# The second output projection as two pairs of column chunks with seven block products each

## The chip, the cores and the metric

The kernel runs on one core of one Trainium2 chip, as one launch. The metric is the device time of that launch in microseconds (us), given as the median of several executions. The profile comes from one more execution, recorded by the hardware profiler; its own time stands beside its span below.

## The reference, cut to what matters

Two transformer blocks run one after the other on 256 tokens of width 2048, in float32. The change touches only this step of the second block, and its result feeds the feed-forward layer behind it:

```
merged = gate_a * (y_a @ w_branch_a) + gate_b * (y_b @ w_branch_b)   # 256 x 2048
x = x + merged @ w_out                                               # 256 x 2048 times 2048 x 2048
x = x + swiglu(rms_norm(x, norm_ffn), w_gate_up, w_down)
```

## The kernel before, in words

Every matrix product is made in float32 precision from three matmuls in a faster format. A weight is split into a high part (`whi`, written by ScalarE with a copy that rounds) and the rest (`wlo`, written by VectorE as raw minus high part). The activations are split in the same way and are the stationary operand. A product of one 128-row tile is then high·high + high·low + low·high, three matmuls of 512 columns into one bank of PSUM.

The unit of work is a *piece*: 256 rows by 512 columns of a weight (128 partitions x 1024 elements). The helper `piece` issues 12 matmuls for it: 2 row tiles (`k`) x 2 token tiles (`i`) x 3. Pieces are numbered through the whole kernel by `g`. Their high and low parts live in a ring of four slots, `whi[:, g % 4]` and `wlo[:, g % 4]`. Three counters order them: `hi_ready` (ScalarE has made the high part of piece g), `lo_ready` (VectorE has made the low part) and `piece_used` (TensorE is through with it). ScalarE waits for `piece_used >= g - 3` before it writes the high part of piece g, so both splitting engines run at most some three pieces ahead of TensorE. The raw weights arrive in four units `raw[:, u]` of 1 MB, two pieces each; SyncE issues the load of a unit when VectorE is through with both pieces that it held (`quad`).

Each engine has its own program, written out by hand in one order. Work beside the splits is hooked in after a numbered piece j of a block of eight (a *block* is one column chunk of 512 columns: 8 pieces over the 2048 rows). The second output projection (`Q_WO2`) is four such blocks, c = 0 to 3, that alternate between the two pairs of accumulator banks, `acc[1]` and `acc[0]`. Around it:

- before it, the last mix block (`Q_MIX + 7`, products with the branch weights) ends in `acc[0]`; VectorE's `branch_b(3)` (L573) multiplies that result by a gate and adds it to `gates`, after piece 2 of c = 0;
- TensorE transposes results in groups of four 128x128 tiles, two groups before piece 4 of a block (`late`, `LATE`); after piece 6 ScalarE and VectorE turn them into stationary operands (`stat_group`): for the merged activations `mhi`, `mlo`, for the residual `hboth` and `rows_of`;
- `h2_add(c - 1)` (L2175) adds the finished chunk to the residual `xres`, on VectorE after piece 2 of the next block; `h2_squares` (L1621) squares it on ScalarE;
- behind it, two blocks of the feed-forward layer (`Q_FF`), then ten loop bodies. The bodies already make part of their gate and up products as seven block products instead of eight (`into`, `right_sum`, `combine`), with a ring of six slots.

Of the kernel before, what the change touches and what calls it, by code (L numbers as in the profile page):

```python
# [33 lines left out]
P = 128  # L34
D = 2048
KT = D // P
TOK = 256
# [33 lines left out]

ORDER = (("a", 0), ("b", 0), ("g", 0), ("c", 0), ("v1", 0), ("g", 1), ("v2", 0), ("u", 0), ("v3", 0),
# [7 lines left out]
B0 = 8 * Q_BODY  # L80
# [97 lines left out]
LATE.update({Q_WO2 + 1 + c: G_H2 + 2 * c for c in range(4)})  # L178
# [29 lines left out]
def build(nc, t, out):  # L208
# [3 lines left out]
    with ctx:  # L212
# [82 lines left out]
        mlo = place("mlo", [P, KT, TOK], F32R, at=o_r + 16384)  # L295
        bias2 = place("bias2", [P, HEADS2, TOK], at=o_ybuf)
# [35 lines left out]

        def raw_piece(u, half):

            return (raw[:, u] if u < 4 else raw2[:, u - 4])[:, 2 * half:2 * half + 2, :]

        def ring(x, odd):

            slot = (NB * odd + x) % SLOTS
            return (whi[:, slot], wlo[:, slot]) if slot < 4 else (whi2[:, slot - 4], wlo2[:, slot - 4])  # L340
# [79 lines left out]
        tile_done = sem("tile_done")  # L420
        h2_added, h2sq, h2var, h2rstd = sem("h2_added"), sem("h2sq"), sem("h2var"), sem("h2rstd")
# [17 lines left out]
        def use_taken(n):  # L439
# [12 lines left out]
            if n < U_FF:  # L452
                return h2_added, n - U_WO2 + 1
            return (ff_silu, 1)

        def late(pe, q, j, transpose_group, aux_bank, aux_used):
# [3 lines left out]
            for s in (LATE[q], LATE[q] + 1):  # L460
# [17 lines left out]
                else:  # L478
                    pe.wait_ge(h2_added, (s - G_H2) // 2 + 1)
# [28 lines left out]
        def late_slot(w, late, j):  # L508

            return late[:, j] if j < 4 else w[:, j - 4]  # L510
# [62 lines left out]
        def branch_b(dve, chain, c):  # L573
# [4 lines left out]
            chain.after(chain.step(nc.vector.tensor_tensor(gate_now[:], pair[(U_MIX + 3 * c + 2) % 2][:], gate_now[:], ALU.mult)))  # L578
            y = gates[:, :, c * CW:(c + 1) * CW]
            nc.vector.tensor_tensor(y, y, gate_now[:], ALU.add).then_inc(merged, 1)  # L580
# [3 lines left out]
        def _(pe):  # L584
# [438 lines left out]
            for c in range(4):  # L1023
                q, n = Q_WO2 + c, U_WO2 + c
                for j in range(8):
                    g = 8 * q + j
                    late(pe, q, j, transpose_group, aux_bank, aux_used)
                    if c == 0 and j % 2 == 0:
                        pe.wait_ge(stat_ready, G_MERGED + j + 2)
                    if j == 0:  # L1030
                        pe.wait_ge(*use_taken(n - 2))
                    pe.wait_ge(lo_ready, g + 1)
                    piece(g % 4, j == 0, j == 7, acc[n % 2], m_stat, 2 * j)
# [10 lines left out]
            for c in range(2):  # L1044
                q = Q_FF + c
                for j in range(8):
                    g = 8 * q + j
# [144 lines left out]
        def _(sp):  # L1192
# [4 lines left out]
            def quad(q, srcs):  # L1197

                for u in range(4):
                    sp.wait_ge(lo_ready, 8 * (q - 1) + 2 * u + 2)  # L1200
# [75 lines left out]
            for c in range(4):  # L1276
                quad(Q_WO2 + c, column_block(t["w_out_2"][0], c * CW))
            quad(Q_FF, column_block(wgu, 0))
            quad(Q_FF + 1, column_block(wgu, DFF))

            def load(i, what, r, u):
# [8 lines left out]
                elif isinstance(i, int) and i == 0:  # L1290
                    if u >= 4:
                        sp.wait_ge(piece_used, 8 * Q_FF)
                    else:
                        sp.wait_ge(lo_ready, 8 * (Q_FF + 1) + 2 * u + 2)
# [26 lines left out]
        def _(act):  # L1321
            chain = Chain(act, act_steps)

            def split(q, j):

                g = 8 * q + j
# [13 lines left out]
                nc.scalar.activation(whi[:, j % 4], raw[:, j // 2, 2 * (j % 2):2 * (j % 2) + 2, :], ACT.Copy).then_inc(hi_ready, 1)  # L1340
# [266 lines left out]
            for c in range(4):  # L1607
                for half_q in range(2):
                    q = Q_MIX + 2 * c + half_q
                    for j in range(8):  # L1610
# [3 lines left out]
                        if half_q == 1 and j == 3:  # L1614
                            sigmoid_b(act, c)
                        if q in LATE and j == 6:
# [4 lines left out]
            def h2_squares(k):  # L1621
                act.wait_ge(h2_added, k + 1)
# [20 lines left out]
            for c in range(4):  # L1643
                q = Q_WO2 + c
                for j in range(8):
                    split(q, j)
# [948 lines left out]
```

## Time and profile before

| what | value |
|---|---|
| time, median of 3 runs | 1731.69 us (1731.48 to 1732.12) |
| the profiled execution's own time | 1731.04 us |
| its span, first to last instruction | 1729.2 us |
| TensorE busy | 1714.8 us, 99% |
| VectorE busy | 1246.7 us, 72% |
| ScalarE busy | 953.1 us, 55% |
| second output projection, first to last matmul | 939.39 to 1030.06 us |

PE is TensorE's matmul side, PEld its weight loads, DVE is VectorE, ACT ScalarE, SP SyncE. Lines such as L1783 are lines of the kernel file. Times in the timeline count from the first instruction. A timeline row can join several instructions of one kind: then its duration runs from the first one's start to the last one's end, and the count stands behind it. An instruction that follows another on its engine without a wait starts a little before the end that the profile gives for the other.

### The profile page before, as it was taken

Reading aid. Unit: us, or ns where it says so; the run is one execution under the profiler, and the core shown is the slowest. Engines: PE = TensorE matmul, PEld = TensorE weight load, DVE = VectorE, ACT = ScalarE, POOL = GpSimd, SP = SyncE. Lnnn points to the kernel's source line nnn. Section 1 sums busy time; section 2 is a strip of 40 time slices with the busy share of each in tenths; the row PEclk is TensorE's granted clock in tenths of the full one; section 3 lists DMA queues with packets and bytes.
Section 4 is the critical chain, followed back from the end, with each engine's and each line's share of the span. In section 5 each row is a group of like instructions: output and inputs, shape, how many; then the busy total and the mean of one; then the engine's idle time right before and its main releaser. Section 6 shows DMA issues by size and latency. Waiting matters only on the chain.

```text
span 1729.2 us, 22918 instructions
## 1 busy us (share of the span) xinstructions
PE 1714.8 (99%) x8641; PEld 1439.5 (83%) x8641; DVE 1246.7 (72%) x1534; ACT 953.1 (55%) x1335; POOL 167.2 (10%) x183
## 2 busy tenths in 40 slices
PE   9999999999999999999999999999999999999998
PEld 8998778888788887888888888788888888888886
DVE  6555765455666667455555567999999999999997
ACT  6334566544553444444444556666666666666663
POOL 1004373000000024000000000011001001001100
PEclk9999999999999999999999999999999999999999
DMA  9754434355586545465665555588688769768871
GB/s 311 244 170 140 147 125 143 123 196 194 159 267 191 169 145 166 148 196 191 194 195 190 177 193 195 193 246 260 233 235 243 240 197 269 247 197 258 249 259 51
DMA packets 198706, 343.45 MB, mean 199 GB/s; under 512 B 6752, under 2 KB 59616, under 8 KB 198112
## 3 DMA queue, kind: packets, MB, share of 16 engines
q1 hardware_dynamic: 186032, 319.49, 55.1%
q0 software_dynamic: 9792, 18.88, 6.0%
q10 hardware_dynamic: 2800, 3.96, 0.7%
q8 instruction: 55, 0.90, 0.2%
q14 instruction: 27, 0.22, 0.0%
HBM read 321.34 MB, written 2.10 MB: 187 GB/s over the span
## 4 chain that ended last, share of the span: by engine, by line
PE 88%; DVE 7%; issue 2%; ACT 2%; POOL 1%; DMA 0%; POOLq 0%; DVEq 0%; ACTq 0%
PE acc L622 12%; PE acc L624 12%; PE acc L623 12%; PE acc L664 5%; PE acc L1073 4%; PE acc L1075 4%; PE acc L1074 4%; PE acc L1087 4%; PE acc L1089 4%; PE acc L1088 4%; DVE wlo L2266 3%; PE acc L665 3%; PE acc L652 2%; PE acc L653 2%; PE acc L651 2%
## 5 line engine op out<-in xcount | busy, mean ns | idle before, releaser
L1783 DVE TENSOR_TENSOR wlo<-raw,whi 128x1024 fp32r<-128x1024 f32 x341 | 422.7, 1241 | 351.2 <-ACT whi L1340 348.0
L1340 ACT ACTIVATE whi<-raw 128x1024 fp32r<-128x1024 f32 x341 | 360.4, 1059 | 322.8 <-PE acc L624 215.7
L1698 ACT ACTIVATE whi<-raw 128x1024 fp32r<-128x1024 f32 x330 | 341.8, 1057 | 169.5 <-PE acc L1075 60.1
L2266 DVE TENSOR_TENSOR wlo<-raw,whi 128x1024 fp32r<-128x1024 f32 x330 | 393.1, 1220 | 33.8 <-ACT whi L1698 31.6
L622 PE MATMUL acc<-whi,hboth 128*128 128x512 f32 x432 | 170.9, 396 | 0.0
L624 PE MATMUL acc<-whi,hboth 128*128 128x512 f32 x432 | 168.4, 390 | 0.0
L623 PE MATMUL acc<-wlo,hboth 128*128 128x512 f32 x432 | 168.3, 390 | 0.0
L664 PE MATMUL acc<-hboth,whi 128*128 128x512 f32 x384 | 135.8, 398 | 0.0
L1087 PE MATMUL acc<-whi,fhi 128*128 128x512 f32 x320 | 124.8, 390 | 1.2 <-DVE xres L2202 1.1
L1088 PE MATMUL acc<-wlo,fhi 128*128 128x512 f32 x320 | 124.5, 389 | 0.0
L1089 PE MATMUL acc<-whi,flo 128*128 128x512 f32 x320 | 124.5, 389 | 0.0
L665 PE MATMUL acc<-hboth,wlo 128*128 128x256 f32 x384 | 106.8, 278 | 0.0
L622 PEld LDWEIGHTS acc<-whi,hboth 128*128 128x128 f32 x432 | 81.1, 188 | 18.4 <-issue 1.5
L2540 POOL DMA_DIRECT2D xres<-down x36 | 43.4, 1206 | 544.9 <-ACT down L1705 444.6
L624 PEld LDWEIGHTS acc<-whi,hboth 128*128 128x128 f32 x432 | 81.1, 188 | 17.2
L623 PEld LDWEIGHTS acc<-wlo,hboth 128*128 128x128 f32 x432 | 81.2, 188 | 16.2
L1073 PE MATMUL acc<-whi,hboth 128*128 128x512 f32 x240 | 94.4, 393 | 0.1
L1075 PE MATMUL acc<-whi,hboth 128*128 128x512 f32 x240 | 93.5, 390 | 0.0
L1074 PE MATMUL acc<-wlo,hboth 128*128 128x512 f32 x240 | 93.4, 389 | 0.0
L651 PE MATMUL acc<-xboth,whi 128*128 128x272 f32 x320 | 92.5, 289 | 0.4 <-DVE wlo L1783 0.4
L652 PE MATMUL acc<-xboth,whi 128*128 128x272 f32 x320 | 92.5, 289 | 0.0
L653 PE MATMUL acc<-xboth,wlo 128*128 128x272 f32 x320 | 92.2, 288 | 0.0
(378 smaller groups left out, 3540.6 us busy)
## 6 DMA issues: line engine op xcount, KB each, us to landing
raw<-w_in SPq DMA_DIRECT2D x112, 1024.0 KB, 5.2
raw<-w_gate_up SPq DMA_DIRECT2D x88, 1024.0 KB, 7.0
raw<-w_down SPq DMA_DIRECT2D x44, 1024.0 KB, 5.2
raw<-w_out SPq DMA_DIRECT2D x32, 1024.0 KB, 5.1
xres<-down POOLq DMA_DIRECT2D x36, 512.0 KB, 8.9
raw<-w_branch_a SPq DMA_DIRECT2D x8, 1024.0 KB, 5.2
raw<-w_branch_b SPq DMA_DIRECT2D x8, 1024.0 KB, 5.1
raw<-w_in SPq DMA_DIRECT2D x5, 512.0 KB, 8.3
```

The source lines that it names most:

```text
L622: nc.tensor.matmul(banks[i][:], sh, hi, start=start, stop=False)
L623: nc.tensor.matmul(banks[i][:], sh, lo, start=False, stop=False)
L624: done = nc.tensor.matmul(banks[i][:], sl, hi, start=False, stop=stop)
L664: nc.tensor.matmul(o.rearrange("p (s t) -> p s t", t=TOK), hi, both[:, :, kt, 0:TOK], start=kt == 0, stop=False)
L1073: nc.tensor.matmul(bank[:], sh, hi[:, k], start=x == FIRST[q[0]] and k == 0, stop=False)
L1087: nc.tensor.matmul(banks[i][:], sh, hi[:, k], start=start, stop=False)
L1088: nc.tensor.matmul(banks[i][:], sh, lo[:, k], start=False, stop=False)
L1089: done = nc.tensor.matmul(banks[i][:], sl, hi[:, k], start=False, stop=stop)
L1340: nc.scalar.activation(whi[:, j % 4], raw[:, j // 2, 2 * (j % 2):2 * (j % 2) + 2, :], ACT.Copy).then_inc(hi_ready, 1)
L1698: nc.scalar.activation(ring(x, odd)[0], raw_piece(u, half), ACT.Copy).then_inc(hi_ready, 1)
L1783: nc.vector.tensor_tensor(wlo[:, j % 4], raw[:, j // 2, 2 * (j % 2):2 * (j % 2) + 2, :], whi[:, j % 4].bitcast(F32), ALU.subtract).then_in ...
L2266: nc.vector.tensor_tensor(lo, raw_piece(UNIT[what, r], half), hi.bitcast(F32), ALU.subtract).then_inc(lo_ready, 1)
```

## The change

The four blocks of the second output projection become two *pairs* of column chunks (left and right), 19 pieces each (`PAIR`). In each pair, the first 512 rows of both chunks are taken as a 2x2 arrangement of blocks: two token tiles by two halves of the rows on the activation side (A11, A12, A21, A22), two halves of the rows by two chunks on the weight side (B11, B21, B12, B22). Their product is made from seven block products instead of eight: `a`, `v1`, `v2`, `b`, `v3`, `c`, `v4`, each one piece with one token tile (6 matmuls). The remaining rows stay as they were: twelve pieces `L2` to `L7`, `R2` to `R7` with 12 matmuls each.

- VectorE makes four sums of activations once (`merged_sums`, after piece 1 of the last mix block, when `hboth` has been read for the last time), which ScalarE and VectorE split (`mshi`, `mslo`).
- VectorE makes four sums of weights per pair (`pair_sum`), in place in the raw units.
- The sums over products are formed in the accumulator banks: ScalarE copies bank left[0] into left[1] after `a` (`seed`), and copies right[0] into an SBUF tile `q5` after `v1` (`keep_q5`); VectorE writes right[0] and right[1] as `q5 - left[1]` after `v2` and after `v3` (`correct`). Later products accumulate on top.
- `v1` is the second product of a pair and the first that writes the right pair of banks. It waits for VectorE to have taken what they held: in the first pair `branch_b(3)`'s multiplication (`branch_taken`), in the second the first half of `h2_add(1)`.
- `branch_b(3)`'s addition becomes a step of its own (`last_merge`, after piece 8 of the first pair). The transposes of the last merged groups come before piece 8 of the first pair; those of the residual chunks before pieces 16 (first pair), 8 and 16 (second pair), with their `stat_group`s after pieces 11 and 18.

The core of the diff (`...` marks what is left out):

```diff
+PAIR = ("a", "v1", "v2", "b", "v3", "c", "v4") + tuple(("L", n) for n in range(2, 8)) + tuple(("R", n) for n in range(2, 8))
+PAIR_LOADS = (("L", 0), ("R", 0), ("L", 1), ("L", 2), ("L", 3), ("R", 1), ("R", 2), ("R", 3))
+PAIR_LAST = (6, 5, 8, 10, 12, 14, 16, 18)
+PAIR_LATE = ({8: G_MERGED + 6, 16: G_H2}, {8: G_H2 + 2, 16: G_H2 + 4})
+H2_DONE = (1, 3, 4, 5)
...
 # TensorE
+            def pair_part(g, bank, stat, i, start=False, last=True):
+                for k in range(2):
+                    hi, lo = whi[:, g % 4, k, :], wlo[:, g % 4, k, :]
+                    sh, sl = stat(k, i)
+                    nc.tensor.matmul(bank[:], sh, hi, start=start and k == 0, stop=False, skip_group_check=True)
+                    nc.tensor.matmul(bank[:], sh, lo, start=False, stop=False, skip_group_check=True)
+                    done = nc.tensor.matmul(bank[:], sl, hi, start=False, stop=k == 1, skip_group_check=True)
+                if last:
+                    done.then_inc(piece_used, 1)
...
+                if op == "a":
+                    pair_part(g, left[0], stat, 0, start=True)
+                elif op == "b":
+                    pair_part(g, left[0], tiles_from(stat, 2), 0)
+                elif op == "c":
+                    pair_part(g, right[0], sum_of(hi, lo, 3), 0)
+                elif op == "v1":
+                    pair_part(g, right[0], sum_of(hi, lo, 0), 0, start=True)
+                elif op == "v2":
+                    pair_part(g, left[1], sum_of(hi, lo, 1), 0)
+                elif op == "v3":
+                    pair_part(g, left[1], sum_of(hi, lo, 2), 0)
+                elif op == "v4":
+                    pair_part(g, left[1], tiles_from(stat, 2), 1)
...
+                    if op == "v1":
+                        if p == 0:
+                            pe.wait_ge(branch_taken, 1)
+                            pe.wait_ge(m_ready, 1)
+                        else:
+                            pe.wait_ge(h2_added, 2)
+                    if op == "v2":
+                        pe.wait_ge(seeded, p + 1)
+                    if op == "v3":
+                        pe.wait_ge(corrected, 2 * p + 1)
+                    if op == "v4":
+                        pe.wait_ge(corrected, 2 * p + 2)
...
 # ScalarE
+            def pair_hi(base, when, p, x):
+                g, op = base + x, PAIR[x]
...
+                if op in ("v1", "v2", "v3", "v4"):
+                    act.wait_ge(pair_sums, 4 * p + {"v1": 1, "v3": 2, "v2": 3, "v4": 4}[op])
+                act.wait_ge(piece_used, g - 3)
+                nc.scalar.activation(whi[:, g % 4], pair_raw(x), ACT.Copy).then_inc(hi_ready, 1)
+            def seed(base, left):
+                act.wait_ge(piece_used, base + 1)
+                nc.scalar.activation(left[1], left[0], ACT.Copy).then_inc(seeded, 1)
+            def keep_q5(base, p, right):
+                act.wait_ge(piece_used, base + 2)
...
+                nc.scalar.activation(q5[:], right[0], ACT.Copy).then_inc(q5_kept, 1)
...
 # VectorE, last mix block
+            def merged_sums():
+                dve.wait_ge(piece_used, 8 * (Q_MIX + 7))
...
 # VectorE, pairs
+            def correct(base, p, step, left, right):
+                dve.wait_ge(piece_used, base + (3, 5)[step])
+                dve.wait_ge(q5_kept, p + 1)
+                nc.vector.tensor_tensor(right[step], q5[:], left[1], ALU.subtract).then_inc(corrected, 1)
+
+                for x in range(NP):
+                    pair_lo(base, x)
+                    if x == 0:
+                        pair_sum("v1", when, p)
+                        pair_sum("v3", when, p)
+                    if x == 1:
+                        pair_sum("v2", when, p)
+                    if x == 2:
+                        pair_sum("v4", when, p)
+                        if p == 0:
+                            branch_b(dve, chain, 3)
+                        else:
+                            h2_add(1)
+                    if x == 4:
+                        correct(base, p, 0, left, right)
+                    if x == 6:
+                        correct(base, p, 1, left, right)
+                    if p == 0 and x == 8:
+                        last_merge(dve)
+                    if x == 11:
+                        stat_group(PAIR_LATE[p][8])
+                        stat_group(PAIR_LATE[p][8] + 1)
+                    if x == 16:
+                        h2_add(2 * p)
+                    if x == 18:
+                        stat_group(PAIR_LATE[p][16])
+                        stat_group(PAIR_LATE[p][16] + 1)
...
 # SyncE
+                for m, (side, r) in enumerate(PAIR_LOADS):
+                    sp.wait_ge(lo_ready, base - 8 + 2 * m + 2 if m < 4 else base + PAIR_LAST[m - 4] + 1)
+                    sp.dma_start(raw[:, m % 4], sides[side][r].rearrange("(k p) n -> p k n", p=P)).then_inc(raw_in[m % 4], 16)
```

The other edits renumber pieces, semaphore counts and ring slots for the 38 pieces where 32 stood.

## Rows read from the trace of the kernel before

**Rows 1.** The page, part 1: busy time of each engine

```profile
PE 1714.8 (99%) x8641; PEld 1439.5 (83%) x8641; DVE 1246.7 (72%) x1534; ACT 953.1 (55%) x1335; POOL 167.2 (10%) x183
```

**Rows 2.** Windows: stretch, its length, then busy us and instruction count per engine

```profile
939.39:1030.06 90.67, 90.67 (x417) 75.39 (x416) 52.37 (x56) 47.35 (x70) 0.00 (x0) 1.00 0.55 183
```

**Rows 3.** Waits of PE over the span: total us, times, longest

```profile
PE acc L1087 <- DVE xres L2202: 1.1, 1, 1.1
```

**Rows 4.** Timeline of PE where the projection begins: start us, us, instruction

```profile
939.17 0.39 PE L624 MATMUL acc<-whi,bboth 128*128 128x512 f32 x1
939.39 0.39 PE L622 MATMUL acc<-whi,mhi 128*128 128x512 f32 x1
```

**Rows 5.** Timeline of ACT and DVE around the same moment

```profile
931.50 1.06 ACT L1340 ACTIVATE whi<-raw 128x1024 fp32r<-128x1024 f32 x1 [1.71 <-PE acc L624]
...
932.59 1.23 DVE L1783 TENSOR_TENSOR wlo<-raw,whi 128x1024 fp32r<-128x1024 f32 x1 [1.44 <-ACT whi L1340]
...
939.69 1.23 DVE L578 TENSOR_TENSOR gate_now<-acc,gate_now 128x1024 f32<-128x1024 f32 x1 [0.16 <-PE acc L624]
```

**Rows 6.** Timeline of DVE and ACT in the first loop body of the feed-forward layer

```profile
1068.86 1.22 DVE L2276 TENSOR_TENSOR raw<-raw 128x1024 f32<-128x1024 f32 x1
...
1077.78 1.22 DVE L2281 TENSOR_TENSOR raw<-raw 128x1024 f32<-128x1024 f32 x1
...
1079.03 2.02 ACT L1698 ACTIVATE whi<-raw 128x1024 fp32r<-128x1024 f32 x2 [1.29 <-DVE raw L2281]
...
1081.19 3.49 DVE L2266 TENSOR_TENSOR wlo<-raw,whi 128x1024 fp32r<-128x1024 f32 x3
```

**Rows 7.** Timeline from the transposes in c = 1 to the next chunk boundary

```profile
972.97 1.03 PE L742 MATMUL aux<-start_c,xres 128*128 128x128 f32 x8
973.76 0.48 PE L622 MATMUL acc<-whi,mhi 128*128 128x512 f32 x1
...
976.48 1.11 ACT L1340 ACTIVATE whi<-raw 128x1024 fp32r<-128x1024 f32 x1
...
977.61 1.23 DVE L1783 TENSOR_TENSOR wlo<-raw,whi 128x1024 fp32r<-128x1024 f32 x1
...
984.93 1.23 DVE L2179 TENSOR_TENSOR xres<-acc,xres 128x1024 f32<-128x1024 f32 x1 [0.34 <-PE acc L624]
```

**Rows 8.** Instructions of 512 columns that read a bank: duration ns min/median/max

```profile
L2291 DVE TENSOR_TENSOR fgate<-acc,sq x10: 682/684/689, 1114.2 to 1672.2; 128x512 f32<-128x512 f32 x10
...
L1727 ACT ACTIVATE sq<-acc x10: 578/579/582, 1111.8 to 1669.9; 128x512 f32<-128x512 f32 x10
```

**Rows 9.** Timeline of DVE and PE at the one wait of Rows 3

```profile
1686.96 1.22 DVE L2202 TENSOR_TENSOR xres<-acc,xres 128x1024 f32<-128x1024 f32 x1
...
1688.23 0.50 PE L1087 MATMUL acc<-whi,fhi 128*128 128x512 f32 x1 [1.09 <-DVE xres L2202]
...
1689.74 0.39 PE L1087 MATMUL acc<-whi,fhi 128*128 128x512 f32 x1
```

**Rows 10.** The page, part 6: DMA issues, KB each, median us to landing

```profile
raw<-w_out SPq DMA_DIRECT2D x32, 1024.0 KB, 5.1
```

**Rows 11.** Timeline of DVE and ACT in the last mix block, and four small sums

```profile
913.49 1.23 DVE L1783 TENSOR_TENSOR wlo<-raw,whi 128x1024 fp32r<-128x1024 f32 x1 [1.44 <-ACT whi L1340]
...
920.62 1.06 ACT L1340 ACTIVATE whi<-raw 128x1024 fp32r<-128x1024 f32 x1 [0.57 <-PE acc L624]
...
1027.70 0.42 DVE L2222 TENSOR_TENSOR sraw<-rows_of 128x256 f32<-128x256 f32 x1
...
1028.95 0.42 DVE L2225 TENSOR_TENSOR sraw<-rows_of,sraw 128x256 f32<-128x256 f32 x1
```

**Rows 12.** Windows at the end of the kernel (columns as in Rows 2; the granted clock is third from last), and the first matmuls

```profile
1722.00:1723.00 1.00, 0.25 (x3) 0.05 (x1) 0.83 (x4) 0.12 (x1) 0.00 (x0) 1.00 0.00 0
...
1724.00:1725.00 1.00, 0.00 (x0) 0.00 (x0) 0.75 (x2) 0.70 (x1) 0.22 (x1) 0.57 0.00 0
...
L854 PE MATMUL acc<-zeros 128*128 128x512 f32 x11 | 5.1, 647 | 1.5 <-DVE zeros L1908 1.5
```

More of the change, by code:

```diff
@@ L508, in late_slot @@
         def late_slot(w, late, j):
-            return late[:, j] if j < 4 else w[:, j - 4]
+            return late[:, j] if j < 4 else w[:, (j + SHIFT) % 4]
         def h1_part_done(i, kt, first, groups):
@@ L1660, in _ @@
                 for j in range(8):
-                    split(q, j)
+                    split(q, j, B_FF + 8 * c)
+                    if c == 0 and j == 1:
+                        h2_squares(2)
                     if q in LATE and j == 6:
@@ L2175, in h2_add @@
             def h2_add(c):
-                dve.wait_ge(piece_used, 8 * (Q_WO2 + c) + 8)
-                x = xres[:, :, c * CW:(c + 1) * CW]
+                dve.wait_ge(piece_used, B_WO2 + NP * (c // 2) + (NP if c % 2 else 13))
+                cs = slice(c * CW, (c + 1) * CW)
+                if c == 1:
+                    for i in range(TT):
+                        nc.vector.tensor_tensor(xres[:, i, cs], acc[(U_WO2 + c) % 2][i], xres[:, i, cs], ALU.add).then_inc(h2_added, 1)
+                    return
+                x = xres[:, :, cs]
                 nc.vector.tensor_tensor(x, pair[(U_WO2 + c) % 2][:], x, ALU.add).then_inc(h2_added, 1)
@@ L2202, in down_add, with pair_lo @@
                 nc.vector.tensor_tensor(x, pair[(1 + m) % 2][:], x, ALU.add).then_inc(down_added, 1)
-            for c in range(4):
-                q = Q_WO2 + c
-                for j in range(8):
-                    split(q, j)
-                    if c == 0 and j == 2:
-                        branch_b(dve, chain, 3)
-                    if c and j == 2:
-                        h2_add(c - 1)
-                    if q in LATE and j == 6:
-                        stat_group(LATE[q])
-                        stat_group(LATE[q] + 1)
+            def pair_lo(base, x):
+                g = base + x
+                dve.wait_ge(hi_ready, g + 1)
+                nc.vector.tensor_tensor(wlo[:, g % 4], pair_raw(x), whi[:, g % 4].bitcast(F32), ALU.subtract).then_inc(lo_ready, 1)
@@ new lines, in pair_sum @@
+            def pair_sum(kind, when, p):
+                b11, b21, b12, b22 = (raw[:, m, 2 * half:2 * half + 2, :] for m in range(2) for half in range(2))
+                if kind == "v1":
+                    dve.wait_ge(raw_in[1], 16 * (when + 1))
+                    nc.vector.tensor_tensor(b11, b11, b12, ALU.add).then_inc(pair_sums, 1)
+                if kind == "v3":
+                    nc.vector.tensor_tensor(b12, b12, b22, ALU.add).then_inc(pair_sums, 1)
+                if kind == "v2":
+                    dve.wait_ge(pair_sums, 4 * p + 1)
+                    nc.vector.tensor_tensor(b11, b11, b22, ALU.add).then_inc(pair_sums, 1)
+                if kind == "v4":
+                    dve.wait_ge(pair_sums, 4 * p + 3)
+                    nc.vector.tensor_tensor(b11, b11, b21, ALU.add).then_inc(pair_sums, 1)
@@ L2234, in _ @@
                 for j in range(8):
[L2235 removed]
+                    split(q, j, B_FF + 8 * c)
                     if c == 0 and j == 2:
```

176 lines of the change are left out of this document (130 added, 46 removed).

## The prediction

> **What bounds the kernel now.** I read the page first. TensorE is busy for 1714.8 us of 1729.2, VectorE for 72%, ScalarE for 55% [rows 1]: whatever takes a matmul away or makes TensorE wait shows in full, and work added to the other two engines shows only where TensorE comes to wait for it. The windows say the same of the stretch in question: 90.67 us long, 90.67 busy, with VectorE working 52.37 and ScalarE 47.35 of it [rows 2]. In TensorE's list of waits the longest of the second block is 1.1 us, once, near the end [rows 3]; none lies in the projection. So the reader should see a stage in which TensorE never waits, and VectorE has 38 us to spare *on average*. The question is whether it has them at the moment when the new products want them.
>
> **What is removed.** A pair had 16 pieces of 12 matmuls, 192; it now has 7 of 6 and 12 of 12, 186. Two pairs save 12 matmuls. Their pace is 0.227 us: the block of 384 matmuls and 32 transposes takes 90.67 us [rows 2], and two starts lie 0.22 apart [rows 4]; a wave of 8 transposes takes 0.79 to the next matmul [rows 7], so (90.67 - 4 x 0.87) / 384 = 0.227, with 0.08 for the slower first matmuls behind each wave. That is **-2.72 us**. A piece is 2.72 us of TensorE, a single product 1.36. The four waves of transposes stay four.
>
> **What is added off the path.** Per pair: three more splits (ScalarE 1.06, VectorE 1.23 each [rows 5]), four weight sums of 1.22 on VectorE [rows 6], two bank copies on ScalarE, two corrections on VectorE. Back to back, VectorE's 1024-element instructions follow every 1.135 us: three take 3.49 [rows 6]. In total some 20 us more of VectorE, which the 38 would hold. They are not spread, though: around the seven singles VectorE must do 2 x 1.135 us where TensorE needs 1.36.
>
> *Activation sums.* After the split that starts at 913.49 [rows 11] VectorE waits for the end of the block before, eight pieces before 939.39, so until 917.9. Then come one 1024-element sum (1.23) and four small ones (1027.70 to 1029.37, 1.67 us [rows 11]), until 920.85 (ScalarE and VectorE split them by 925.4, long before `v1`). The next split ends at 922.0; TensorE wants it at 917.6 + 5.44 = 923.05. Margin 1.0 us, no wait. ScalarE's split for it follows its instruction at 920.62 [rows 11]; by the piece after 927 both engines are on their old times. Cost 0; were it late by more than 1.0 us, it would show one for one.
>
> *Loads.* A load lands in 5.1 us [rows 10]. The unit reused inside a pair (L3 into unit 0) is free with the split of `v4`, about 9.6 us after the pair starts, and lands at 14.8. Its split leads TensorE by three pieces and is due at 14.8; TensorE wants it at 23.7. Cost 0, up to landings of some 12 us. SyncE's queue has nothing else in it.
>
> **The first pair.** Everything hangs on `v1`, the second product: it may write `acc[0]` only when VectorE has multiplied the last branch result out of it. Before, that bank was wanted eight pieces and a wave of transposes (22.6 us) after the start of the projection, now 1.36 us after. VectorE's queue ahead of that multiplication, with the rows' own times: ScalarE's split 931.50, VectorE's 932.59 to 933.82 [rows 5]. Sum v1 to 934.95, sum v3 to 936.08. ScalarE can split v1 only from 934.98 (0.03 after the sum, as 1077.78 + 1.22 to 1079.03 [rows 6]), to 936.04; VectorE's low part 936.07 to 937.30; sum v2 to 938.43; ScalarE's split of v2 to 939.52; low part 939.55 to 940.78; sum v4 to 941.9; only now the multiplication, 941.83 to 943.06. Before, it ran at 939.69 [rows 5], 0.30 after TensorE's last matmul of the block. TensorE starts 0.05 after such a release: 1686.96 + 1.22 = 1688.18, start 1688.23 [rows 9]. So `v1` starts at 943.11 where `a` is through at 939.39 + 1.36 = 940.75: **+2.36 us**.
>
> **The second pair.** `v1` waits for the first half of `h2_add(1)`, at the same place of VectorE's queue, and the queue starts later. ScalarE and VectorE first do the `stat_group`s behind the transposes. After transposes at 972.97 ScalarE's next weight split starts at 976.48 and lasts 1.11; VectorE's follows at 977.61 [rows 7]. The next chunk began 11.66 us after the transposes (984.93 - 0.30 [rows 5, 7]) with four pieces between. Now only three pieces (16, 17, 18) lie between, so the pair starts at 11.66 - 2.72 = 8.94 after them. Counted from that start: low part of `a` -4.30 to -3.07; sum v1 to -1.95, sum v3 to -0.81; ScalarE v1 -1.92 to -0.86; low part to 0.40; sum v2 to 1.52; ScalarE v2 1.55 to 2.61; low part to 3.87; sum v4 to 4.99; first half of the addition 4.91 to 5.59 (0.68 for a bank of 512 [rows 8]); `v1` at 5.64 instead of 1.36: **+4.28 us**.
>
> Behind either wait the first matmuls are slow: from 1688.23 six intervals take 1.51 instead of 1.36 [rows 9], +0.15 each time, **+0.30**.
>
> **The rest of the singles.** After `v1` both queues are short. In the first pair, with `v2` from 944.6, `correct` ends 0.4 us before `v3` may start and the second one 0.3 us before `v4`. That takes 0.58 and 0.68 us for instructions that *write* a bank, which the trace of before does not show; the rows are of reads [rows 8]. Lower bound: these rows, cost 0. Upper bound: the 1024-element instructions, 1.06 and 1.22 [rows 5, 6]. Then the two corrections are late by 0.1 and 0.5 us, with restarts 0.9 per pair, 1.9 in all. I take the rows of 512 elements, the same size. Behind the singles TensorE takes 2.72 us a piece again, and the others need 2.3 at most, a split and one instruction more. `last_merge` stands after piece 8 and ends 13.6 us after the start of the first pair; the transposes that wait for it are due at 14.6, so they cost nothing; were it late, they would hold the pieces behind them. In the two feed-forward blocks VectorE is 2.7 us late at first and catches up before their fourth piece; their own wait positions are unchanged.
>
> **Sum.** -2.72 + 2.36 + 4.28 + 0.30 = **+4.2 us**. Against the profiled execution: span 1729.2 to 1733.4, own time 1731.0 to 1735.3. The median of the runs is 0.65 above that execution, so 1731.7 + 4.2 = **1735.9 us**, +0.24%. A difference of 0.2% (3.5 us) is about what a measurement of this kernel can tell from none.
>
> **Rivals.**
> 1. *The pause lowers TensorE's clock.* The granted clock is still full from 1722 to 1723, where the last matmuls end (busy 0.25 of 1.00), and averages 0.57 from 1724 to 1725 [rows 12]: it fell to the lower level, 1.2 GHz, 2.0 us after TensorE went idle. The wait of 1.1 us did not do it. Both new waits are longer than 2.0 us. At the lower level eleven matmuls of the start take 5.1 us [rows 12], 0.44 each, until about 5.4 us after the first. If that happens behind the second wait, half of 5.4 us is lost: +2.7, **1738.6**; behind both, 1741.3. Against it: the one fall in the trace has no work behind it, and whether a pause of 4.3 us does the same is not seen. I give it 0.17. The Trainium skill, "TensorE: Matmul & The Clock Gate" (section on why this matters for your kernels), says that a gap between bursts of matmuls takes TensorE back to half rate; by that rule the longer of the two waits could do it and 1738.6 would be the time. It is the rule that speaks against this change.
> 2. *The lead of the splitting engines covers both waits* (the order on VectorE lets the release come before `v1` is due, since it idles 38 us in the stage). Then the multiplication starts at 939.69 as before and ends at 940.92, `v1` starts 0.2 us late, and with the restart it is 1731.7 - 2.7 + 0.4 = **1729.4**, no slower than before. It decides from the point where two of the seven instructions ahead of the release are gone (941.83 - 939.69 = 2.14 us), and in the second pair four. Against it: the queue is strictly in order, and each link of it has a row. 0.06.
> 3. *Only one of the waits is there*, the second above all, since it hangs on where the transposes stand: without the second 1731.5, without the first 1733.4. 0.10.
> 4. *Writes to a bank cost double* and the corrections are late too: **1737.8**. 0.07.
> 5. The forecast, both waits and nothing else, 1735.9: 0.60.
>
> **How the numbers follow.** The forecast's own range is 1735.2 to 1736.8, from 0.2 us of uncertainty at each of the four handovers and 0.3 in the median; about 0.9 of its chance lies above the bound of 1735.2. Slower by over 0.2%: 0.54 + 0.17 + 0.07, less something for mixtures with rival 3, 0.73. Faster by over 0.2% would need 1728.2, more than all removed matmuls give: 0.02. The rest, 0.25. The range takes in rival 4, the single fall of the clock and the upper half of rival 3: 1733.2 to 1738.8; outside lie rival 2, the wait of the first pair alone, and two falls.
>
> **What the profile after should show.** TensorE's list of waits: `v1` twice, once released by L578's successor in `branch_b` (about 2.3 us), once by the halved `h2_add` (about 4.2 us). VectorE with no idle time over 0.1 us between the low part of `v2` and the release, and about 1.2 us of idle before that low part, waiting for ScalarE, in each pair. The corrections ending before `v3` and `v4` are due. The projection 4.2 us longer than 90.67. The granted clock at full from end to end; if it is not, rival 1. The prediction is wrong if VectorE reaches the release with less in front of it than seven instructions, if the chain sum, split, low part of `v1` and `v2` runs closer together than 3.5 us a link, or if the corrections hold TensorE.

## The result and the profile after

| | before | after |
|---|---|---|
| time, median (lowest to highest) | 1731.59 us (1731.06 to 1732.88, 6 runs) | 1737.93 us (1737.52 to 1739.36, 6 runs) |
| the profiled execution's own time, its span | 1731.04, 1729.2 us | 1737.69, 1735.9 us |

The ratio is 1.0037 (95% interval 1.0024 to 1.0050): the change makes the kernel 6.3 us slower, where 4.2 were forecast.

The page after, part 1. The busy time of TensorE [rows 1] has grown by 0.1 us although 12 matmuls are gone, so some matmuls must have run slower:

```profile
PE 1714.9 (99%) x8629; PEld 1439.0 (83%) x8629; DVE 1267.7 (73%) x1559; ACT 962.5 (55%) x1346; POOL 167.3 (10%) x183
```

Its waits: total us, times, longest:

```profile
PE acc L1086 <- DVE xres L2351: 4.1, 1, 4.1
PE acc L1086 <- DVE gate_now L626: 2.2, 1, 2.2
```

The windows after: the projection (answers to [rows 2]), then single microseconds around the second wait. The third column from the end is the granted clock:

```profile
939.35:1036.56 97.21, 90.94 (x406) 74.74 (x405) 67.52 (x72) 55.49 (x81) 0.00 (x0) 0.96 0.51 175
989.00:990.00 1.00, 0.00 (x0) 0.00 (x0) 1.00 (x2) 1.00 (x3) 0.00 (x0) 0.85 0.00 0
990.00:991.00 1.00, 0.00 (x0) 0.00 (x0) 1.00 (x2) 0.77 (x1) 0.00 (x0) 0.50 0.00 0
995.00:996.00 1.00, 1.00 (x4) 0.81 (x3) 0.00 (x0) 0.93 (x1) 0.00 (x0) 0.50 0.00 0
996.00:997.00 1.00, 1.00 (x5) 0.82 (x4) 0.17 (x1) 0.11 (x1) 0.00 (x0) 0.73 0.00 0
```

TensorE's timeline, from the beginning of the projection (compare [rows 4]) and at both waits:

```profile
939.35 0.39 PE L1086 MATMUL acc<-whi,mhi 128*128 128x512 f32 x1
...
940.48 0.39 PE L1088 MATMUL acc<-whi,mlo 128*128 128x512 f32 x1
943.07 0.50 PE L1086 MATMUL acc<-whi,mshi 128*128 128x512 f32 x1 [2.20 <-DVE gate_now L626]
943.41 0.39 PE L1087 MATMUL acc<-wlo,mshi 128*128 128x512 f32 x1
...
986.96 0.39 PE L1088 MATMUL acc<-whi,mlo 128*128 128x512 f32 x1
991.42 0.80 PE L1086 MATMUL acc<-whi,mshi 128*128 128x512 f32 x1 [4.07 <-DVE xres L2351]
992.01 0.63 PE L1087 MATMUL acc<-wlo,mshi 128*128 128x512 f32 x1
992.44 0.63 PE L1088 MATMUL acc<-whi,mslo 128*128 128x512 f32 x1
...
996.63 0.39 PE L1086 MATMUL acc<-whi,mhi 128*128 128x512 f32 x1
```

The projection has become 97.21 - 90.67 = 6.5 us longer, the span 6.7. Read off these rows, in the forecast's terms: the products saved, -2.72. `v1` of the first pair starts at 943.07 where it was due at 940.48 + 0.23 = 940.71: +2.36. That of the second starts at 991.42 instead of 987.19: +4.23. Behind the first wait the first six intervals between matmuls take 1.50 us instead of 1.36 (the first alone 0.34): +0.14. Behind the second, twelve intervals take 996.63 - 991.42 = 5.21 us instead of 2.72: **+2.49**. The sum is +6.50, 0.04 from the 6.54 measured.

The last term is nearly all the clock; a slow restart like the first one's would be 0.14 of it. The windows show it at full until about 989.7 (0.85 of that microsecond), at 0.50, the 1.2 GHz level, from 990 to 996, and back at about 996.5 (0.73). TensorE's last matmul before had ended at 987.35, 2.3 us before the fall. During the low clock matmuls start 0.43 us apart.

VectorE's timeline up to the first release, and the first correction:

```profile
932.54 1.23 DVE L2383 TENSOR_TENSOR wlo<-raw,whi 128x1024 fp32r<-128x1024 f32 x1 [1.45 <-ACT whi L1770]
933.68 1.22 DVE L2390 TENSOR_TENSOR raw<-raw 128x1024 f32<-128x1024 f32 x1
934.82 1.22 DVE L2392 TENSOR_TENSOR raw<-raw 128x1024 f32<-128x1024 f32 x1
936.03 1.23 DVE L2383 TENSOR_TENSOR wlo<-raw,whi 128x1024 fp32r<-128x1024 f32 x1
937.17 1.22 DVE L2395 TENSOR_TENSOR raw<-raw 128x1024 f32<-128x1024 f32 x1
939.52 1.23 DVE L2383 TENSOR_TENSOR wlo<-raw,whi 128x1024 fp32r<-128x1024 f32 x1 [1.13 <-ACT whi L1770]
940.66 1.22 DVE L2398 TENSOR_TENSOR raw<-raw 128x1024 f32<-128x1024 f32 x1
941.80 1.22 DVE L626 TENSOR_TENSOR gate_now<-acc,gate_now 128x1024 f32<-128x1024 f32 x1
...
946.13 0.70 DVE L2404 TENSOR_TENSOR acc<-q,acc 128x512 f32<-128x512 f32 x1 [0.85 <-PE acc L1088]
```

The reader should see the queue as it was written: low part of `a`, sums v1 and v3, low part of `v1`, sum v2, 1.13 us of idling for ScalarE, low part of `v2`, sum v4, and only then the multiplication that sets the bank free, at 941.80 where it ran at 939.69 before [rows 5]. The correction, which writes a bank, takes 0.70 us, as the reads of [rows 8].

### The profile page after: what moved, and what is told of

The parts are those of the page before. It is cut to its first block, busy times and chain, and to the rows that moved or that the text cites. A ratio compares the mean times of both kernels' runs of the same rounds, so it can differ in the third digit from the quotient of the medians.

```text
span 1735.9 us, 22949 instructions
## 1 busy us (share of the span) xinstructions
PE 1714.9 (99%) x8629; PEld 1439.0 (83%) x8629; DVE 1267.7 (73%) x1559; ACT 962.5 (55%) x1346; POOL 167.3 (10%) x183
## 4 chain that ended last, share of the span: by engine, by line
PE 86%; DVE 8%; ACT 2%; issue 2%; POOL 1%; DMA 1%; POOLq 0%; DVEq 0%; ACTq 0%
PE acc L680 10%; PE acc L682 10%; PE acc L681 10%; PE acc L722 5%; PE acc L1184 4%; PE acc L1186 4%; PE acc L1185 4%; PE acc L1198 4%; PE acc L1199 4%; PE acc L1200 4%; DVE wlo L2487 3%; PE acc L723 3%; PE acc L710 2%; PE acc L711 2%; PE acc L709 2%
## 5 line engine op out<-in xcount | busy, mean ns | idle before, releaser
L1936 DVE TENSOR_TENSOR wlo<-raw,whi 128x1024 fp32r<-128x1024 f32 x309 | 383.6, 1243 | 313.1 <-ACT whi L1455 310.4
L1455 ACT ACTIVATE whi<-raw 128x1024 fp32r<-128x1024 f32 x309 | 326.6, 1059 | 281.6 <-PE acc L682 173.1
L1851 ACT ACTIVATE whi<-raw 128x1024 fp32r<-128x1024 f32 x330 | 341.8, 1057 | 166.6 <-PE acc L1186 60.1
L2487 DVE TENSOR_TENSOR wlo<-raw,whi 128x1024 fp32r<-128x1024 f32 x330 | 392.6, 1217 | 34.5 <-ACT whi L1851 32.5
```

Of the source, the lines that this page charges most:

```text
L1455: nc.scalar.activation(whi[:, g % 4], raw[:, j // 2, 2 * (j % 2):2 * (j % 2) + 2, :], ACT.Copy).then_inc(hi_ready, 1)
L1851: nc.scalar.activation(ring(x, odd)[0], raw_piece(u, half), ACT.Copy).then_inc(hi_ready, 1)
L1936: nc.vector.tensor_tensor(wlo[:, g % 4], raw[:, j // 2, 2 * (j % 2):2 * (j % 2) + 2, :], whi[:, g % 4].bitcast(F32), ALU.subtract).then_in ...
L2487: nc.vector.tensor_tensor(lo, raw_piece(UNIT[what, r], half), hi.bitcast(F32), ALU.subtract).then_inc(lo_ready, 1)
```

## The experiments

**Theory**: the two places in VectorE's queue cost 2.4 and 4.2 us, and a clock that falls in the pause costs some 2.5 more. **Rivals**: the lost time is a handover cost of writing accumulators by VectorE and ScalarE (the corrections, the seed), or the clock has nothing to do with the pause. A kernel that is compared with the changed one ran on another chip in most cases, so such differences are taken between the distances of the two from their own "before". In all experiments "before" is the kernel before on the same chip: 1731.82 for the first four kernels, 1731.60 for the next four, 1732.03 for the sums on GpSimd, 1731.94 for the last.

### Keeping TensorE busy in the second wait

```diff
                         else:
+                            for _ in range(18):
+                                nc.tensor.matmul(sbank[0][:], mhi[:, 0, 0:P], mhi[:, 0:2, :], start=True, stop=True)
                             pe.wait_ge(h2_added, 2)
```

The results of these matmuls are used by nothing.

> The changed kernel with 18 more matmuls of 512 columns (into a bank that nobody reads) before the second pair's v1, where TensorE otherwise stands still for 4.2 us; their results are thrown away. Theory: the wait itself costs 4.2 us and stays, since VectorE's queue is untouched, and the pause of TensorE takes its clock to the lower level, which costs 2.5 us more on the 12 matmuls of v1 and v2 (5.21 us in place of 2.72). With TensorE busy the clock stays up: 18 x 0.227 = 4.1 us of the wait is filled, v1 starts as before and the time falls by 2.5 us, from 1737.9 to 1735.4. Rival, the level of the clock is incidental and the 2 us beyond the forecast were lost elsewhere: the time stays at 1737.9 or rises, since work was added.

Measured: 1736.66 (1735.92 to 1739.37, 6 runs), ratio 1.0031 (1.0019 to 1.0043). The profiled execution took 1735.92 at full clock throughout; three of six stood at 1735.9 to 1736.2, the others up to 3.2 us higher, with a mean clock of 0.998 for the core instead of 0.999. So the second wait's clock loss is gone in the profiled execution, but the median is only 1.5 us closer to the kernel before (4.8 instead of 6.3 us above it) where 2.5 were expected, and some loss is left in other executions. The fifth experiment fills the other wait too.

### One sum less in front of the release

```diff
                     if x == 2:
-                        pair_sum("v4", when, p)
                         if p == 0:
                             branch_b(dve, chain, 3)
                         else:
                             h2_add(1)
+                        pair_sum("v4", when, p)
```

> The changed kernel with the sum for v4 moved behind the release of the right banks, in both pairs. Theory, the release is late by what stands ahead of it in VectorE's queue: both waits shrink by one instruction, 1.13 us, to 1.2 and 3.1 us; the time falls by 2.3 us to 1735.6 if the clock still falls in the pause of 3.1 us, and by 4.8 us to 1733.1 if it does not. Rival, the waits are set by ScalarE's splits of v1 and v2 or by the bank itself: the waits stay at 2.4 and 4.2 and the time at 1737.9.

Measured: 1734.99 (1733.60 to 1737.06, 11 runs), ratio 1.0020 (1.0011 to 1.0029). Its waits:

```profile
PE acc L1086 <- DVE xres L2351: 2.9, 1, 2.9
...
PE acc L1086 <- DVE gate_now L626: 1.1, 1, 1.1
```

Each wait is shorter by one VectorE instruction, 1.1 to 1.2 us: the order of the queue sets them. The profiled execution (1733.67) has the clock at 1.00 behind the wait of 2.9 us; two of eleven runs stand at 1733.6, the others 0.9 to 3.5 us above, most at a mean clock of 0.998 or 0.997 instead of 0.999. I read this as one pause that is followed by a fall in some executions and not in others.

### The transposes of the residual one piece earlier

The residual's transposes at the end of each pair move from before piece 16 to before piece 15, their operands from behind piece 18 to behind 17, the addition that they need from 16 to 15.

```diff
-PAIR_LATE = ({8: G_MERGED + 6, 16: G_H2}, {8: G_H2 + 2, 16: G_H2 + 4})
+PAIR_LATE = ({8: G_MERGED + 6, 15: G_H2}, {8: G_H2 + 2, 15: G_H2 + 4})
```

> The changed kernel with the last transposes of each pair one piece earlier (before piece 15, their stationary operands after piece 17, the addition to the residual after piece 15), so that four pieces lie behind them as before the change. Theory, the second wait is 2.7 us longer than it need be because both splitting engines are held up by these operands: second wait 4.2 to 1.6 us, first unchanged at 2.4, clock not falling: 1737.9 - 2.6 - 2.5 = 1732.8. Rival, the seven instructions ahead of the release set the second wait alone: it stays above 4 us and the time within 0.5 us of 1737.9.

Measured: 1736.98 (1734.2 to 1738.49, 10 runs), ratio 1.0024 (1.0015 to 1.0034). The waits are 2.2 and 2.5, not 1.6 for the second: VectorE now has the split of piece 18 behind the operands too, one instruction of 1.14 us that the expectation forgot. The median is 4.2 us above the expected 1732.8; that instruction explains 1.1 of it. The profiled execution is the slowest, and its windows show something the change's own profile did not:

```profile
944.00:945.00 1.00, 0.18 (x1) 0.19 (x2) 1.00 (x2) 0.19 (x1) 0.00 (x0) 1.00 0.00 0
945.00:946.00 1.00, 1.00 (x5) 0.82 (x5) 1.00 (x2) 0.00 (x0) 0.00 (x0) 1.00 0.00 0
946.00:947.00 1.00, 1.00 (x4) 0.70 (x3) 1.00 (x1) 0.19 (x1) 0.00 (x0) 0.50 0.00 0
948.00:949.00 1.00, 1.00 (x4) 0.81 (x3) 0.00 (x0) 0.35 (x1) 0.00 (x0) 0.50 0.00 0
949.00:950.00 1.00, 1.00 (x5) 0.79 (x5) 0.63 (x2) 0.57 (x1) 0.00 (x0) 0.80 0.00 0
```

After the *first* wait, of 2.2 us, matmuls resume at 944.82 at full clock, and the clock falls at about 946.0, when TensorE is busy again, until 949.4. It fell behind the second wait as well, again only after the matmuls had resumed, at 993.8 where they resumed at 993.17. Each of the two falls costs about 1.6 us.

### One more instruction in front of the first release

A VectorE sum of 1024 elements that nothing needs stands ahead of `branch_b(3)` in the first pair.

> The changed kernel with one more addition of 1024 elements on VectorE ahead of the first pair's release (into a scratch tile that is no longer read). Theory: the first wait grows by 1.2 us, from 2.4 to 3.6 us. If a pause of 3.6 us is enough to lower TensorE's clock, 2.5 us come on top behind the first pair too: 1741.6 with the clock low in both places, 1739.1 if only in the second. Rival, VectorE has slack here and the extra instruction disappears in it: 1737.9.

Measured: 1741.77 (1740.61 to 1745.41, 5 runs), ratio 1.0060 (1.0046 to 1.0074). The first wait grows from 2.2 to 3.5 us, 1.3 for an instruction of 1.22. The kernel is now 10.0 us above the kernel before instead of 6.3, so the instruction costs 3.6. The clock is part of the rest: it falls behind the first wait too, at 945.7, where the changed kernel had it at full in its profile, and is back at 949.1. The windows where it falls:

```profile
945.00:946.00 1.00, 1.00 (x6) 0.77 (x5) 1.00 (x2) 0.00 (x0) 0.00 (x0) 0.86 0.00 0
946.00:947.00 1.00, 1.00 (x4) 0.81 (x3) 0.80 (x1) 0.41 (x1) 0.00 (x0) 0.50 0.00 0
```

That is a low stretch of 3.4 us, half as long as the changed kernel's behind the second wait, and by the intervals between matmuls it costs 1.6 us, not the 2.5 that the expectation put in. The low stretch behind the second wait meets 0.4 us more of work than in the changed kernel. 1.3 + 1.6 + 0.4 leave 0.3 of the 3.6 us open, so that the expected 1741.6 was met is in part luck.

### Both waits filled

9 and 18 throwaway matmuls, in front of the two waits.

> The changed kernel with matmuls whose results are thrown away in both waits: 9 before the first pair's v1 (2.04 of 2.4 us) and 18 before the second's (4.1 of 4.2 us). Theory: with only the second wait filled the median was 1736.7 and single runs went up to 1739.4, because the clock may also fall behind the first wait; with both filled it stays up in every run: median 1735.6, runs within 0.8 us of it, 3.9 us above before, which are the two waits less the 12 matmuls. Rival, the scatter comes from something else: median 1736.7 or more, runs again over 3 us apart.

Measured: 1735.63 (1735.25 to 1736.47, 11 runs), ratio 1.0022 (1.0013 to 1.0031). The windows: the projection, around the end of the first wait, around that of the second:

```profile
939.61:1034.46 94.85, 94.70 (x433) 78.08 (x431) 67.53 (x72) 55.36 (x81) 0.00 (x0) 1.00 0.52 179
943.00:946.00 3.00, 2.85 (x13) 2.18 (x13) 2.54 (x3) 0.97 (x2) 0.00 (x0) 1.00 0.00 0
990.00:994.00 4.00, 4.00 (x18) 3.02 (x17) 4.00 (x5) 1.67 (x4) 0.00 (x0) 1.00 0.00 0
```

TensorE's timeline at the second wait:

```profile
987.48 4.24 PE L1131 MATMUL scores<-mhi 128*128 128x512 f32 x18
991.71 0.50 PE L1086 MATMUL acc<-whi,mshi 128*128 128x512 f32 x1
```

This is the experiment that separates pause from clock. The releases come when they came before, the waits are as long, but TensorE does idle work in them: the projection is 94.85 - 90.67 = 4.2 us longer instead of 6.5, and the eleven runs lie within 1.2 us. The 2.3 us between 1737.93 and 1735.63, and the 2.4 between the two projections, are the clock.

### The eight weight sums left out

The products `v1` to `v4` take raw blocks of the weight instead of sums, so the output differs; all matmuls, splits, copies and corrections are as in the changed kernel, and the releases stand where they stood.

> The changed kernel without the eight sums of weights on VectorE and without ScalarE's waits for them: v1 to v4 are made from the raw halves that lie there, so the projection's values are others; every product, split, copy and correction stays. Theory, these sums and the chain sum, split, low part are what holds the release: it then starts when TensorE leaves the bank, the first wait shrinks to 0.2 us, the second vanishes, the clock stays up: -2.7 + 0.4, so 1729.4. Rival, the single products are held anyway (by seed, q5 and the corrections, or by three more splits per pair): still 1731.5 or more.

Measured: 1729.03 (1728.54 to 1729.85, 11 runs), ratio 0.9982 (0.9973 to 0.9991). TensorE has no wait at all in the stretch. So the seven products, the seed, the copy and the corrections cost next to nothing beside the matmuls (0.2 us before the first `v1`); the saving of 2.7 us is real, and the sums' place on VectorE takes it away.

### The release before the low part of `v2`

```diff
                     if x == 1:
                         pair_sum("v2", when, p)
+                        if p == 0:
+                            branch_b(dve, chain, 3)
+                        else:
+                            h2_add(1)
                     if x == 2:
                         pair_sum("v4", when, p)
-                        if p == 0:
-                            branch_b(dve, chain, 3)
-                        else:
-                            h2_add(1)
```

> The changed kernel with the release of the right banks moved ahead, behind the sum for v2 and in front of the low part of v2, in both pairs; the sum for v4 follows after that low part. Theory: the release is early, but VectorE's queue is still too full for the single products, so smaller waits appear further on: first pair 0.1 before v1 and together 0.8 at b and v3, second pair 0.7 before v1 and together 1.2 at v2, b and v3. No pause is over 1 us, the clock stays up: 1.1 us above before, 1732.9. Rival, the order was the whole fault and VectorE has room: waits gone, 2.3 us below before, 1729.5.

Measured: 1732.79 (1732.35 to 1733.52, 11 runs), ratio 1.0005 (0.9996 to 1.0014): 5.1 us better than the change, by moving one call. Some 2.3 of them are the clock, which stays at full in the profiled execution. VectorE's timeline in the first pair:

```profile
937.47 1.22 DVE L2395 TENSOR_TENSOR raw<-raw 128x1024 f32<-128x1024 f32 x1
939.95 1.23 DVE L626 TENSOR_TENSOR gate_now<-acc,gate_now 128x1024 f32<-128x1024 f32 x1 [1.26 <-PE acc L682]
941.09 1.22 DVE L2383 TENSOR_TENSOR wlo<-raw,whi 128x1024 fp32r<-128x1024 f32 x1
942.22 1.22 DVE L2398 TENSOR_TENSOR raw<-raw 128x1024 f32<-128x1024 f32 x1
```

TensorE's waits:

```profile
PE acc L1086 <- DVE wlo L2383: 0.8, 2, 0.4
...
PE acc L1086 <- DVE xres L2351: 0.6, 1, 0.6
```

The gap in which VectorE idled for ScalarE now holds the release, which comes as soon as TensorE has ended the block before. The price is that low parts become late by 0.4 us, twice; in the second pair the release itself is still late by 0.6 us, and `v2` waits 0.3 us for ScalarE's seed. With the transposes before piece 14 (and their operands behind 16) on top:

> As the run with the release ahead, and the last transposes of each pair two pieces earlier (before piece 14, addition to the residual after piece 14, operands after piece 16). Theory: both pairs now behave like the first pair of that run, 0.1 at v1 and 0.8 to 1.1 at b and v3, which eats what 12 matmuls save: 1731.8, no different from before. Rival, as above: 2.3 us below before, 1729.5.

Measured: 1731.94 (1731.42 to 1732.25, 11 runs), ratio 1.0000 (0.9991 to 1.0009). The wait for `h2_add` is gone, that for low parts stays (0.9 us, two times).

### Two of the four sums on GpSimd

The kernel with the early release and the transposes before piece 14, with sums v3 and v4 of each pair on GpSimd, which is idle in this stage.

> As the run with the release ahead and the transposes two pieces earlier, but the weight sums for v3 and v4 are made by GpSimd, which is idle in this stage; those for v1 and v2 stay on VectorE. A sum of 1024 elements should take GpSimd 2.1 to 3.7 us, twice its 1.0 to 1.8 for 510 and 512 elements, and there are 4.5 us or more for each. Theory, VectorE's throughput around the single products is what is left: without 2.3 us per pair the waits at b and v3 vanish, 0.2 at v1 remains: 2.3 us below before, 1729.4. Rival, the two engines slow each other down at the memory, or the chain sum, split, low part binds on ScalarE's side: 1731.5 or more.

Measured: 1735.78 (1734.93 to 1737.82, 11 runs), ratio 1.0023 (1.0014 to 1.0032). It is 3.75 us above the kernel before on its chip, where the same kernel with these sums on VectorE was 0.34 above: 3.4 us *slower*. The rival holds. VectorE's and GpSimd's timelines:

```profile
933.71 1.22 DVE L2391 TENSOR_TENSOR raw<-raw 128x1024 f32<-128x1024 f32 x1
936.05 2.44 DVE L2384 TENSOR_TENSOR wlo<-raw,whi 128x1024 fp32r<-128x1024 f32 x1 [1.13 <-ACT whi L1771]
...
935.00 2.40 POOL L2751 TENSOR_TENSOR raw<-raw 128x1024 f32<-128x1024 f32 x1 [249.24 <-DVE raw L2391]
942.11 3.31 POOL L2753 TENSOR_TENSOR raw<-raw 128x1024 f32<-128x1024 f32 x1 [4.70 <-DVE wlo L2384]
```

VectorE's split, 1.23 us elsewhere, takes 2.44 when it starts while GpSimd adds, and ends 1.1 us after GpSimd does: the two take turns. The Trainium skill, "GPSIMD Engine Reference" (section on specifications), lists GpSimd's SBUF interfaces as shared with VectorE, contending where a VectorE instruction has two SBUF inputs; the split has two, and the trace agrees.

The delay reaches TensorE through the first correction, which stands behind these splits. `v3` waits for it in both pairs, and the clock falls behind both waits. TensorE's wait, and the windows behind the second of them:

```profile
PE acc L1087 <- DVE acc L2400: 3.7, 2, 1.9
...
995.00:996.00 1.00, 0.79 (x3) 0.67 (x4) 1.00 (x2) 0.50 (x1) 0.00 (x0) 1.00 0.00 0
996.00:997.00 1.00, 1.00 (x4) 0.79 (x3) 1.00 (x2) 0.00 (x0) 0.00 (x0) 0.56 0.00 0
```

The pauses are 1.8 and 1.9 us long, shorter than any other in these experiments that a fall followed. Matmuls resume at 947.16 and 995.21 at full clock, the clock falls at 948.3 and 996.1 and is back 3.4 us later; each fall costs about 1.6 us. So the 3.4 us come from two waits of about 2 us and from falls of the clock, less the waits for low parts that are gone; how often both falls happen in the other executions is not known.

### The sums made ahead

Sum v1 gets a buffer of its own instead of being made in place, so that sums v1 and v3 no longer have to wait for the low part of `a`. The last transposes stand before piece 14, as in the run before the one with GpSimd; that part of the edit is left out here.

```diff
+        v1sum = place("v1sum", [P, 2, CW], at=o_h + 8192)
...
+                        if (c, half_q, j) == (3, 1, 7):
+                            pair_sum("v1", Q_WO2, 0)
+                            pair_sum("v3", Q_WO2, 0)
...
                     if x == 0:
-                        pair_sum("v1", when, p)
-                        pair_sum("v3", when, p)
-                    if x == 1:
                         pair_sum("v2", when, p)
+                    if p == 0 and x == 17:
+                        pair_sum("v1", when + 2, 1)
+                    if p == 0 and x == 18:
+                        pair_sum("v3", when + 2, 1)
                     if x == 2:
-                        pair_sum("v4", when, p)
                         if p == 0:
                             branch_b(dve, chain, 3)
                         else:
                             h2_add(1)
+                    if x == 3:
+                        pair_sum("v4", when, p)
```

> The sum v1 gets a buffer of its own, so that the sums v1 and v3 of the first pair are made behind the last split of the block before, those of the second pair behind the splits of pieces 17 and 18 of the first pair; sum v2 is made from it behind the low part of a, the release stands behind the low part of v2 as in the changed kernel, sum v4 behind the low part of v3. The last transposes stand before piece 14 and their operands behind piece 16. By my theory (VectorE's order around the singles is all that costs, and a pause of under 1 us does not touch the clock) no product waits for more than about 0.5 us and the saving of 2.7 us stays, less some 0.4 for what remains: 1729.4 where the kernel before takes 1731.7. Rival A: the sums made ahead only move the lateness to the pieces of the block before and to the last pieces of the first pair, TensorE waits there for low parts by some 1 to 2 us, and it takes 1731 to 1732, as the kernel with the early release and the transposes before piece 14 did (1731.9). Rival B: the clock falls all the same with no pause above 1 us, 1732 or more.

Measured: 1729.88 (1729.49 to 1731.11, 11 runs), ratio 0.9987 (0.9978 to 0.9996): faster than the kernel before, by 2.1 us. The window of the projection:

```profile
939.56:1028.34 88.78, 88.72 (x406) 72.83 (x404) 66.70 (x71) 55.22 (x80) 0.00 (x0) 1.00 0.57 195
```

VectorE's timeline at the first release:

```profile
934.81 1.22 DVE L2330 TENSOR_TENSOR raw<-v1sum,raw 128x1024 f32<-128x1024 f32 x1
935.96 1.22 DVE L2406 TENSOR_TENSOR wlo<-v1sum,whi 128x1024 fp32r<-128x1024 f32 x1
938.19 1.23 DVE L2406 TENSOR_TENSOR wlo<-raw,whi 128x1024 fp32r<-128x1024 f32 x1 [1.02 <-ACT whi L1773]
939.86 1.22 DVE L629 TENSOR_TENSOR gate_now<-acc,gate_now 128x1024 f32<-128x1024 f32 x1 [0.44 <-PE acc L685]
```

The release now waits for TensorE, not TensorE for it. The stretch is 1.9 us shorter than before; 0.8 of the 2.72 are lost in it still. TensorE's matmuls show no wait there, but its weight loads wait 0.8 us in all for corrections, three times, and 0.5 us for the first release, which may be it; that was not tried.

## Why the prediction went as it did

- **The number and the case**: the measured 1737.93 lies in the stated range, 1733.2 to 1738.8, only because the range took in rival 1. The forecast's own case, 1735.2 to 1736.8, does not hold it.
- **Saved products, -2.72**: right. The kernel without sums, in which TensorE never waits, is 2.57 us under the kernel before.
- **First wait, +2.36**: 2.36. **Second wait, +4.28**: 4.23. The chain of sum, split, low part ran at 3.49 us a link, and the idle gap before the low part of `v2` was the forecast's 1.2 us in both pairs (1.13, 1.12). Moving one sum or one release moved the waits by what those instructions take.
- **Activation sums, loads, seed, corrections, `last_merge` at nothing**: right; no wait of the matmuls names them, and leaving only the weight sums out gives the whole saving. Rival 4 is out: a bank's write takes 0.70 us at most.
- **Rival 2** is out as stated: VectorE's 38 idle microseconds in the stage did not help. The experiment with the early release shows that they could, once the order lets them.
- **Restarts, +0.30**: 0.14 behind the first wait, where 0.15 was put; behind the second it can't be told from the clock.
- **The step that failed**: "The granted clock at full from end to end". The forecast was the case with both waits and nothing else, 1735.9; the kernel with both waits filled shows that case, 1735.63. The changed kernel itself is rival 1, one fall of the clock at the second wait, sized +2.7 and measured +2.49 in the trace (a restart of some 0.14 in it) and 2.3 between the medians. I gave it 0.17 although the only row on the matter [rows 12] had the clock fall 1.9 us after TensorE went idle (I wrote 2.0), and both waits were forecast to be longer. In the changed kernel it fell 2.3 us into the wait. My reason against it, that the fall of [rows 12] had no work behind it, was no evidence that a pause with work behind it goes otherwise. By the Trainium skill, "TensorE: Matmul & The Clock Gate" (section on why this matters for your kernels), gaps between bursts send TensorE back to half rate; the trace agrees for the wait of 4.1 us, and shows none for the wait of 2.2 us in the same execution.

What stays open: of the profiled executions, some show a fall behind pauses of 1.8 to 2.5 us and others none behind pauses of 2.2 and 2.9 us. What decides it was not found. That it differs from execution to execution of one kernel is read from their times and mean clocks alone. These are rounded to 0.001 (1.7 us) and do not always fit: one run of the changed kernel took 1737.66 us at a mean clock of 0.999, and the kernel before, which has no such pause, has single runs of 1734.35 and 1736.12 us at 0.997. How often the changed kernel loses its clock behind the first wait too was not measured: its two slowest runs, 1739.06 and 1739.36, would fit with a second fall of 1.6 us.

## What to carry to other kernels

Count the instructions that stand between a bank's last use and its release on the engine that reads it out, in the order written, not the engine's idle share: here seven instructions stood there, and moving the call ahead of two of them gave back 5.1 us of 6.3, 2.3 of it through the clock. When a wait as long as these (1.8 us and more) on TensorE can't be avoided, reckon with the price of a clock fall on top (here 1.6 us where it fell with TensorE back at work, 2.5 where it fell in the wait), or give TensorE throwaway matmuls for the time. No fall followed the waits of 1.2 us and less in these profiles. In-place sums tie work to the last read of the raw data; a buffer of its own for the first sum let the work go into the idle time that the averages had promised.

## What was unexpected of the hardware

- The clock can fall *after* the pause, with TensorE at work again: 1.2 us after the matmuls resumed in the kernel with the transposes one piece earlier, following a pause of 2.2 us, and as late behind a pause of 1.8 us in the kernel with GpSimd's sums. A low stretch lasted 3.4 us there, and 6.8 us behind the pause of 4.1 us, of which 5.1 had matmuls in them.
- A pause of 2.9 us, longer than these, was not followed by a fall in the profiled execution of the kernel with sum v4 behind the release.
- GpSimd's addition and VectorE's split, each with two inputs in SBUF, took turns: 1.23 us became 2.44.
